# A decoder trunk on one core: Strassen's seven products for the merge of the three branches and for the down projection, and norms with one token per partition

## The chip, the cores and the metric

The kernel runs on one core of a Trainium2 chip. The metric is the device time of one execution in microseconds (us). All arithmetic is in f32.

## The reference, cut to what matters

Two layers of a decoder trunk for 512 prompt tokens and 8 sample tokens, D_MODEL 1024, D_FF 2816. What the change touches is the norm at the head of each layer and everything from the merge of the three branches (A, B, C) to the end of the layer:

```
h = rms_norm(x, norm_mix)
... the three token mixers make o_a, o_b, o_c from h @ w_in
m_a, m_b, m_c = split(sigmoid(h @ w_in[merge columns]), 3)
merged = m_a * (o_a @ w_rg_out) + m_b * (o_b @ w_gla_out) + m_c * (o_c @ w_nsa_out)
x = x + merged @ w_out
h = rms_norm(x, norm_ffn)
x = x + (silu(h @ w_ffn_gate) * (h @ w_ffn_up)) @ w_ffn_down
```

rms_norm divides each token by the root of the mean of its squares, plus 1e-6, and multiplies by a gain per channel.

## The kernel before, in words

Activations stand transposed: 1024 channels are 8 tiles of 128 partitions, and the free axis holds the 520 tokens (`xT`, `hT`, `oaT`, `obT`, `ocT`, each 128 x 8 x 520). PSUM holds 260 f32 tokens of a tile in a bank, so a tile is computed as two halves in a pair of banks. The two layers are one loop; a layer is a row of blocks, and between two blocks all engines meet. Weights come in slabs of 2 MB (1024 rows by 512 columns) into `ring`, which has three slots; SyncE's queue issues a slab's DMA (`load_slab`, L317) once TensorE has done with the slab three before it.

**Merge and output projection** (block from L2516). `proj_T` (L368) computes one tile of 128 channels by 520 tokens with 16 matmuls: 2 halves by 8 tiles of the inner dimension. There are 48 such tiles a layer: for each half of the columns, each branch and each of 4 tiles a gate tile from `hT` and an output tile from `oaT`, `obT` or `ocT`. ScalarE takes the sigmoid of the gate tile (L2549), VectorE multiplies the output tile by it (L2564) and adds it into `MG` (L2568). When all is merged, TensorE computes the 8 tiles of `w_out`; VectorE adds each into `xT` (L2571), ScalarE squares it (L569), and TensorE sums the squares over the channels with a matrix of ones, two matmuls a tile (`sum_tile`, L562), one tile behind.

**Norm.** The sums of squares stand in one pair of banks, the same on all 128 partitions. VectorE makes the means of them (L577), ScalarE the roots (L573), VectorE the reciprocals (L581) and the eight tiles of `hT` (L583), all as 128 x 520 operations. The norm at the head of a layer runs by the same lines in the first block of the layer, where squares and sums alternate.

**FFN** (block from L2580). Gate and up projection already go by Winograd's form of Strassen's algorithm. A step makes 2 tiles of channels by 520 tokens, with seven products P1 to P7 of 4 matmuls each (`product`, L457) instead of eight. VectorE makes four sums of weight blocks for each step, one step ahead (L467 to L472), and once four sums of blocks of `hT` (L477 to L482); ScalarE copies P1 from PSUM (L2615), and VectorE adds the products up (`add_products`, L489) as they end. Products go round the eight banks, so a product waits for the addition that read the bank eight products before. There are 22 steps a layer, then the down projection by plain matmuls (L2600), 352 program matmuls a layer, and VectorE adds each of 8 tiles into `xT` (L2652).

The order that sets how products and additions interleave is

```python
ORDER = ("P1", "P2", "P5", "P6", "P3", "P7", "P4")
```

The profile counts an f32 matmul of the program as two instructions of TensorE, with two weight loads.

## Time and profile before

| what | value |
|---|---|
| median of 3 runs | 3939.35 us (3935.71 to 3940.05) |
| the profiled execution's own time | 3938.83 us |
| its span, first to last instruction | 3937.2 us |
| TensorE busy | 3640.8 us, 92% of the span |
| VectorE busy | 1405.0 us, 36% |
| ScalarE busy | 761.7 us, 19% |
| mean granted TensorE clock | 0.945 |

The profile is of one execution. A row of the timeline gives the start in us from the first instruction, how long the merged instructions last together, engine, line, operation, output and inputs by the program's names, shapes, how many instructions (x), and in brackets how long the engine had been idle and what ended that. PEld is TensorE's weight load, DVE is VectorE, ACT is ScalarE. A line ending in "xN" with several instructions tells their common stretch, not one duration.

### The profile page before, as it was taken

The page shows a single profiled execution, that of the slowest core. Times are in us where ns is not written, and L with a number is a line of the kernel's source. Part 1 is how long each engine was busy: PE and PEld are TensorE (multiplying, and loading weights), DVE is VectorE, ACT ScalarE, POOL GpSimd, SP SyncE. Part 2 cuts the span into 40 slices and gives each one's busy share as a digit, 9 for nine tenths or more (in the row PEclk, how much of TensorE's full clock was granted, in tenths as well). Part 3 has the DMA queues.
Part 4 walks back from the last instruction along what each step waited for, and adds up shares of the span by engine and source line. Part 5 has one row for each costly group of instructions (what it writes and reads, how often), then busy time and mean ns, then how long its engine had stood idle before and what let it go on. Part 6 is the DMA issues. An engine that isn't in the chain of part 4 may idle for free. (4 is left out here: it accounts for less than half of the span.)

```text
span 3937.2 us, 47054 instructions
## 1 busy us (share of the span) xinstructions
PE 3640.8 (92%) x18570; PEld 2840.1 (72%) x18570; DVE 1405.0 (36%) x3043; ACT 761.7 (19%) x1564; POOL 285.9 (7%) x396
## 2 busy tenths in 40 slices
PE   6899898989789999999988988989887899999999
PEld 5777765755558887888877677556555688878888
DVE  4714514557300013442055164235662000144411
ACT  2312323146200001000032132221551000010000
POOL 0000011024200000000000000110342000000000
PEclk9999988989889999999999998889898999999999
DMA  4111353120542221222122104522206321212121
GB/s 141 46 65 44 101 153 118 59 114 1 169 136 71 86 83 46 86 75 91 38 100 67 64 27 131 161 75 75 97 16 192 113 77 65 86 65 86 65 102 38
DMA packets 222171, 336.97 MB, mean 86 GB/s; under 512 B 56614, under 2 KB 122386, under 8 KB 217210
## 3 DMA queue, kind: packets, MB, share of 16 engines
q1 hardware_dynamic: 204474, 281.91, 22.1%
q0 software_dynamic: 8064, 43.00, 3.1%
q10 hardware_dynamic: 9408, 8.98, 0.7%
q8 instruction: 151, 2.47, 0.3%
q14 instruction: 74, 0.61, 0.0%
HBM read 313.50 MB, written 37.10 MB: 89 GB/s over the span
## 5 line engine op out<-in xcount | busy, mean ns | idle before, releaser
L368 PE MATMUL pair<-hT,ring 128*128 128x260 f32 (+1 forms) x3648 | 835.2, 390 | 48.3 <-PEq L1419 25.2
L368 PEld LDWEIGHTS pair<-hT,ring 128*128 128x128 f32 (+1 forms) x3648 | 699.6, 192 | 171.6 <-issue 56.7
L383 PE MATMUL pair<-ring,hT 128*128 128x512 f32 (+2 forms) x800 | 311.8, 556 | 5.5 <-PEq L1262 5.5
L2600 PE MATMUL pair<-arena,ring 128*128 128x260 f32 x1408 | 309.1, 383 | 2.7 <-DVE arena L2648 2.7
L2600 PEld LDWEIGHTS pair<-arena,ring 128*128 128x128 f32 x1408 | 267.4, 190 | 44.4 <-DVE arena L2648 3.4
L383 PEld LDWEIGHTS pair<-ring,hT 128*128 128x128 f32 (+1 forms) x800 | 151.8, 212 | 153.4 <-issue 152.8
L2564 DVE TENSOR_TENSOR arena<-pair,arena 128x520 f32<-128x520 f32 x48 | 33.6, 700 | 626.4 <-PE pair L368 626.4
L457 PE MATMUL pair<-obT,oaT 128*128 128x260 f32 x1056 | 246.3, 383 | 0.0
L457 PEld LDWEIGHTS pair<-obT,oaT 128*128 128x128 f32 x1056 | 201.3, 191 | 31.2
L2118 POOL TENSOR_SCALAR arena<-arena 128x128 f32<-128x128 f32 (+3 forms) x256 | 152.4, 611 | 506.5 <-DVE arena L2077 506.5
L457 PE MATMUL pair<-hT,ring 128*128 128x260 f32 x704 | 169.4, 395 | 17.2 <-DVE hT L583 17.2
L457 PEld LDWEIGHTS pair<-hT,ring 128*128 128x128 f32 x704 | 137.8, 196 | 41.4 <-issue 16.4
L1529 PE MATMUL pair<-arena 128*128 128x512 f32 (+1 forms) x320 | 157.4, 578 | 6.6 <-DVE arena L1642 6.6
L489 DVE TENSOR_TENSOR ocT<-ocT,pair 128x260 f32<-128x260 f32 x220 | 91.2, 423 | 199.9 <-PE pair L457 194.5
L1983 ACT ACTIVATE arena<-arena 128x128 f32<-128x128 f32 (+3 forms) x256 | 141.4, 554 | 62.6 <-DVE arena L2037 60.6
L2549 ACT ACTIVATE arena<-pair 128x520 f32<-128x520 f32 x48 | 29.0, 604 | 621.2 <-PE pair L368 621.2
L1514 PEld LDWEIGHTS pair<-con,arena 128*128 128x128 f32 (+1 forms) x640 | 80.0, 153 | 76.4 <-issue 74.7
L880 POOL DMA_DIRECT2D out_p_gla_dram<-arena x8 | 4.6, 577 | 1728.2 <-DVE arena L1184 1728.2
L921 PE MATMUL pair<-hT,ring 128*128 128x260 f32 x512 | 125.6, 389 | 0.0
L2037 DVE CUSTOM_DVE_ANT_0 arena<-pair,con 128x128 f32<-128x128 f32 (+3 forms) x256 | 114.5, 484 | 28.8 <-PE pair L1912 28.6
L2652 DVE TENSOR_TENSOR xT<-pair,xT 128x520 f32<-128x520 f32 x16 | 11.2, 700 | 299.6 <-PE pair L2600 299.6
L368 PE MATMUL pair<-arena,ring 128*128 128x260 f32 x512 | 114.7, 383 | 3.0 <-DVE arena L2568 3.0
(372 smaller groups left out, 4922.5 us busy)
## 6 DMA issues: line engine op xcount, KB each, us to landing
ring<-in_w_in_dram SPq DMA_DIRECT2D x38, 2048.0 KB, 8.6
ring<-in_w_ffn_gate_dram SPq DMA_DIRECT2D x10, 2048.0 KB, 7.8
ring<-in_w_ffn_up_dram SPq DMA_DIRECT2D x10, 2048.0 KB, 7.8
ring<-in_w_ffn_down_dram SPq DMA_DIRECT2D x8, 2048.0 KB, 7.6
out_s_win_kv_dram<-in_cache_win_kv_dram SPq DMA_DIRECT2D x2, 8176.0 KB
...
```

What stands on the lines that cost most here:

```text
L368: last = pe.matmul(pair[o][0:m, half, 0:HA], lhs(k), rhs[:, k, half * HA:(half + 1) * HA], start=(k == 0), stop=(k == nk - 1))
L383: last = pe.matmul(big[0:rows, 0:w], hT[:, k, tt * P:tt * P + rows], slab[:, k, 0:w], start=(k == 0), stop=(k == KT - 1))
L457: last = pe.matmul(step_bank(q, prod), a[:, k, :], b[:, k, :], start=(k == 0), stop=(k == 3))
L489: dve.tensor_tensor(dst, a, step_bank(q, prod), op).then_inc(sem("st_sums"), 1)
L921: last = pe.matmul(pair[proj_pair(key)][:, half, 0:HA], gr[0][:, k, m % 4 * P:(m % 4 + 1) * P], hT[:, k, half * HA:(half + 1) * HA], start ...
L1514: last = pe.transpose(bank[4 + kv][:, g * P:g * P + n], R2[z // 2 % 3][0:n, kv * G + g, :], ident[0:n, 0:n])
L1529: pe.matmul(dst, PH[:, kv, 2 * qt + sp2_, :], src, start=(qt == 0 and sp2_ == 0), stop=(qt == 3 and sp2_ == 1)).then_inc(sem("ct_mm"), 1)
L1983: act.activation(s[:, u, 0:n], s[:, u, 0:n], ACT.Exp, bias=st[:, u:u + 1], scale=-1.0, accum_out=st[:, 4 + u:5 + u]).then_inc(sem("sa_e"), 1)
L2037: dve.tensor_tensor_reduce(out=SC[:, g % NSL, u, 0:n], in0=bank[S_BANK[u]][:, 0:n], in1=dist[:, 384 - i * P:384 - i * P + n], scale=SLOPE[ ...
L2118: pool.tensor_scalar(s, s, stat[:, g % NSL, 4 + u:5 + u], GATE[:, i, k:k + 1], ALU.mult, ALU.mult).then_inc(sem("sa_p"), 1)
L2564: dve.tensor_tensor(two(dst), both(proj_pair(key)), two(SG[i % 3]), ALU.mult).then_inc(sem("proj_read_dve"), 1)
L2600: last = pe.matmul(pair[m][:, half, 0:HA], w[:, k, m * P:(m + 1) * P], FA[:, r + k, half * HA:(half + 1) * HA], start=(r + k == 0), stop=( ...
```

## The change

- Merge and down projection become Strassen steps like those of the FFN: a layer has 24 merge steps (`MERGE_STEPS`), the 22 of gate and up as before, and 12 of the down projection (`DOWN_STEPS`), each the product of one slab of `w_ffn_down` (8, 8 or 6 tiles of rows) with a third of the activations, added straight into `xT`. Step, slab and input set follow from one list; the merge takes the branches one after the other.
- The sums stand in place: `T1` overwrites the block `B12` of its own input (so `input_sums` waits three times), and `stored_sums` builds U2, U5, U3 in the quarters of the destination. `added_sums`, for the down projection, has 11 additions a step, of them 4 of SBUF operands alone. Gates are taken by one 128 x 1040 operation behind the last sum, and the products with them too.
- Input sums are made once for each set: `hT` and `oaT` at the head of the merge, `obT` and `ocT` at steps 8 and 16, `hT` again behind the FFN norm, and three sets of the FFN's activations behind its steps of pairs 3, 7 and 10.
- Norms: VectorE adds up the eight squares (`add_square`), TensorE turns the sum with five matmuls of one column each, so that 128 tokens stand on the partitions; mean, root and reciprocal are 128 x 4 and 8 x 1; five matmuls with the identity spread the reciprocals over the partitions in PSUM (`spread_roots_pe`), from where VectorE reads them for `hT`.

```diff
+    MERGE_STEPS = [(n, hf, br, i) for br in range(3) for hf in range(2) for i in range(2) for n in ("mg", "mo")]
+    FFN_STEPS = [(n, i) for i in range(FT // 2) for n in ("fg", "fu")]
+    DOWN_STEPS = [("fd", hf, r, i) for hf in range(2) for r in range(0, FT, 8) for i in range(2)]
+    STEPS = MERGE_STEPS + FFN_STEPS + DOWN_STEPS
+    NTH = {key: q for q, key in enumerate(STEPS)}
+    SETS = ["hm", "oa", "ob", "oc", "hf", "f0", "f8", "f16"]
...
+    MADE_X = {"T3": 1, "T1": 2, "T2": 3, "T4": 4}
+    STORED = ("U2", "C11", "U5", "C12", "C22", "U3", "C21")
+    ADDED = ("X11", "U2", "C11", "U5", "C12", "X12", "C22", "U3", "X22", "X21", "C21")
...
+    def input_sums(dve, name, inputs):
+        x, xsum = inputs[name]
+        n, done = 4 * SETS.index(name), sem("st_inputs")
+        dve.tensor_tensor(xsum["T3"], input_block(x, "B22"), input_block(x, "B12"), ALU.subtract).then_inc(done, 1)
+        dve.wait_ge(done, n + MADE_X["T3"])
+        dve.tensor_tensor(xsum["T1"], input_block(x, "B12"), input_block(x, "B11"), ALU.subtract).then_inc(done, 1)
+        dve.wait_ge(done, n + MADE_X["T1"])
+        dve.tensor_tensor(xsum["T2"], input_block(x, "B22"), xsum["T1"], ALU.subtract).then_inc(done, 1)
+        dve.wait_ge(done, n + MADE_X["T2"])
+        dve.tensor_tensor(xsum["T4"], xsum["T2"], input_block(x, "B21"), ALU.subtract).then_inc(done, 1)
+    def input_tiles(x, space):
+        kh = x.shape[1] // 2
+        return x, {"T1": input_block(x, "B12"), **{t: space.take(kh, HA) for t in ("T3", "T2", "T4")}}
...
+    def stored_sums(dve, q, t):
+        c_ = quarters_of(t)
+        dve.wait_ge(sem("st_kept"), q + 1)
+        add_product(dve, q, "U2", c_["21"], c_["11"], "P6")
+        add_product(dve, q, "C11", c_["11"], c_["11"], "P2")
+        add_product(dve, q, "U5", c_["22"], c_["21"], "P5", made="U2")
+        add_product(dve, q, "C12", c_["12"], c_["22"], "P3", made="U5")
+        add_product(dve, q, "C22", c_["22"], c_["22"], "P7")
+        add_product(dve, q, "U3", c_["21"], c_["21"], "P7")
+        add_product(dve, q, "C21", c_["21"], c_["21"], "P4", ALU.subtract, made="U3")
+        dve.wait_ge(*sums_done(q, "C21"))
+    def added_sums(dve, q, t, u1, u2, u5):
+        c_, done = quarters_of(t), sem("st_sums")
+        dve.wait_ge(sem("st_kept"), q + 1)
+        dve.tensor_tensor(c_["11"], c_["11"], u1, ALU.add).then_inc(done, 1)
+        add_product(dve, q, "U2", u2, u1, "P6")
+        add_product(dve, q, "C11", c_["11"], c_["11"], "P2", made="X11")
+        add_product(dve, q, "U5", u5, u2, "P5", made="U2")
+        add_product(dve, q, "C12", c_["12"], c_["12"], "P3", made="U5")
+        dve.wait_ge(*sums_done(q, "C12"))
+        dve.tensor_tensor(c_["12"], c_["12"], u5, ALU.add).then_inc(done, 1)
+        add_product(dve, q, "C22", c_["22"], c_["22"], "P7")
+        add_product(dve, q, "U3", u2, u2, "P7")
+        dve.wait_ge(*sums_done(q, "C22"))
+        dve.tensor_tensor(c_["22"], c_["22"], u5, ALU.add).then_inc(done, 1)
+        dve.wait_ge(*sums_done(q, "U3"))
+        dve.tensor_tensor(c_["21"], c_["21"], u2, ALU.add).then_inc(done, 1)
+        add_product(dve, q, "C21", c_["21"], c_["21"], "P4", ALU.subtract, made="X21")
+    def keep_first(act, q, dst):
+        wait_product(act, q, "P1")
+        act.activation(dst, step_bank(q, "P1"), ACT.Copy).then_inc(sem("st_kept"), 1)
...
+    def norm_pe(pe, tag, ms):
+        pe.wait_ge(*normed(tag, "sum", KT - 1))
+        for tt, n in TOKENS:
+            last = pe.matmul(bank[6][0:n, tt:tt + 1], ms[:, tt * P:tt * P + n], ones[:, 0:1], start=True, stop=True)
+        last.then_inc(sem("norm_sum"), 1)
+    def spread_roots_pe(pe, tag):
+        pe.wait_ge(*normed(tag, "ms", 2))
+        for tt, n in TOKENS:
+            last = pe.matmul(bank[4 + tt // NT][:, tt % NT * P:tt % NT * P + n], rstd[0:n, 1, tt:tt + 1].to_broadcast([n, P]),
+                             ident[0:n, 0:n], start=True, stop=True)
...
+    def add_square(dve, tag, k, ms):
+        dve.wait_ge(*normed(tag, "sq", k + 1))
+        if k >= 2:
+            dve.wait_ge(*normed(tag, "sum", k - 1))
+        dve.tensor_tensor(ms, tag_sq[tag][0] if k == 1 else ms, tag_sq[tag][k % 2], ALU.add
+                          ).then_inc(sem("norm_sum"), 1)
...
+    def norm_mean(dve, own, tag):
         dve.wait_ge(*normed(tag, "sum", KT))
...
+        m, b = token_columns(rstd[:, 0, :]), token_columns(bank[6])
+        own.tick(dve.tensor_scalar(m[0], b[0], 1.0 / DM, EPS, ALU.mult, ALU.add))
+        own.wait()
+        dve.tensor_scalar(m[1], b[1], 1.0 / DM, EPS, ALU.mult, ALU.add).then_inc(sem("norm_ms"), 1)
+    def norm_dve(dve, own, tag, gain):
+        dve.wait_ge(*normed(tag, "rt", 2))
+        m, r = token_columns(rstd[:, 0, :]), token_columns(rstd[:, 1, :])
+        own(dve.reciprocal(r[0], m[0]))
+        dve.reciprocal(r[1], m[1]).then_inc(sem("norm_ms"), 1)
+        dve.wait_ge(*normed(tag, "sum", KT + 1))
+        both_banks = pair[2].rearrange("p a n -> p (a n)")[:, 0:TA]
         for k in range(KT):
-            dve.scalar_tensor_tensor(hT[:, k, :], xT[:, k, :], par[:, PR[gain] + k:PR[gain] + k + 1], ms,
+            dve.scalar_tensor_tensor(hT[:, k, :], xT[:, k, :], par[:, PR[gain] + k:PR[gain] + k + 1], both_banks,
...
+                for q in range(len(MERGE_STEPS)):
+                    open_slab(pe, step_slab(q))
+                    for prod in ORDER:
+                        product(pe, q, prod, wsum, inputs)
+                pe.wait_ge(sem("proj_read_dve"), dve_reads(MERGE_STEPS[-1]))
                 for hf in range(2):
                     w = open_slab(pe, f"wo{hf}")
                     for m in range(4):
                         j = 4 * hf + m
                         proj_T(pe, ("wo", j), lambda k: w[:, k, m * P:(m + 1) * P], MG)
...
+                norm_pe(pe, "ffn", ms8)
...
+                for q, (n, hf, br, i) in enumerate(MERGE_STEPS):
+                    if q >= 2 and (n == "mo" or br):
+                        act.wait_ge(sem("proj_read_dve"), dve_reads(MERGE_STEPS[q - 1 - (n == "mo")]))
+                    gate = MGATE if br else MG[:, 4 * hf + 2 * i:4 * hf + 2 * i + 2, :]
+                    keep_first(act, q, gate[:, 0, 0:HA] if n == "mg" else TMP[:, 0, 0:HA])
+                    if n == "mg":
+                        act.wait_ge(*sums_done(q, "C21"))
+                        act.activation(gate, gate, ACT.Sigmoid).then_inc(sem("proj_read_act"), 1)
...
+                weight_sums(dve, 0, wsum)
+                input_sums(dve, "hm", inputs)
+                weight_sums(dve, 1, wsum)
+                input_sums(dve, "oa", inputs)
+                for q, (n, hf, br, i) in enumerate(MERGE_STEPS):
+                    if 1 <= q < len(MERGE_STEPS) - 1:
+                        weight_sums(dve, q + 1, wsum)
+                    if q in (8, 16):
+                        wait_product(dve, q - 1, "P4")
+                        input_sums(dve, ("ob", "oc")[q // 8 - 1], inputs)
+                    merged = MG[:, 4 * hf + 2 * i:4 * hf + 2 * i + 2, :]
+                    gate = MGATE if br else merged
+                    stored_sums(dve, q, gate if n == "mg" else TMP)
+                    if n == "mo":
+                        dve.wait_ge(sem("proj_read_act"), act_reads(("mg", hf, br, i)))
+                        if br == 0:
+                            dve.tensor_tensor(merged, merged, TMP, ALU.mult).then_inc(sem("proj_read_dve"), 1)
+                        else:
+                            dve.tensor_tensor(TMP, TMP, MGATE, ALU.mult).then_inc(sem("merged"), 1)
+                            dve.wait_ge(sem("merged"), 4 * (br - 1) + 2 * hf + i + 1)
+                            dve.tensor_tensor(merged, merged, TMP, ALU.add).then_inc(sem("proj_read_dve"), 1)
                 for j in range(KT):
                     wait_proj(dve, ("wo", j))
                     dve.tensor_tensor(two(xT[:, j, :]), both(proj_pair(("wo", j))), two(xT[:, j, :]), ALU.add
                                       ).then_inc(sem("proj_read_dve"), 1)
+                    if j >= 2:
+                        add_square(dve, "ffn", j - 1, ms8)
+                add_square(dve, "ffn", KT - 1, ms8)
...
+                for q in range(len(MERGE_STEPS), len(STEPS)):
+                    n, *k = STEPS[q]
                     open_slab(pe, step_slab(q))
-                    product(pe, q, "P1", wsum, hT, xsum, made="ffn" if q == 0 else None)
-                    if q == 0:
+                    if q == len(MERGE_STEPS):
+                        product(pe, q, "P1", wsum, inputs, made="ffn")
                         pe.wait_ge(*normed("ffn", "h", KT))
+                    else:
+                        if n == "fd":
+                            pe.wait_ge(sem("proj_read_dve"), dve_reads(("fu", min(k[1] // 2 + 4, FT // 2) - 1)))
+                        product(pe, q, "P1", wsum, inputs)
                     for prod in ORDER[1:]:
...
+                        product(pe, q, prod, wsum, inputs)
...
+                norm_mean(dve, own, "ffn")
+                weight_sums(dve, len(MERGE_STEPS), wsum)
+                norm_dve(dve, own, "ffn", "ffn")
                 dve.wait_ge(*normed("ffn", "h", KT))
-                input_sums(dve, hT, xsum)
-                for q, (n, i) in enumerate(STEPS):
+                input_sums(dve, "hf", inputs)
+                for q in range(len(MERGE_STEPS), len(STEPS)):
+                    n, *k = STEPS[q]
                     if q + 1 < len(STEPS):
                         weight_sums(dve, q + 1, wsum)
...
+                    if n == "fg":
+                        stored_sums(dve, q, GATE)
+                    elif n == "fu":
+                        i, up = k[0], FA[:, 2 * k[0]:2 * k[0] + 2, :]
+                        stored_sums(dve, q, up)
                         dve.wait_ge(sem("proj_read_act"), act_reads(("fg", i)))
...
+                        dve.tensor_tensor(up, up, GATE, ALU.mult).then_inc(sem("proj_read_dve"), 1)
+                        if i in (3, 7, FT // 2 - 1):
+                            dve.wait_ge(sem("proj_read_dve"), dve_reads(("fu", i)))
+                            input_sums(dve, {3: "f0", 7: "f8"}.get(i, "f16"), inputs)
+                    else:
+                        j = 4 * k[0] + 2 * k[2]
+                        added_sums(dve, q, xT[:, j:j + 2, :], *KEPT)
```

TensorE at the end of a layer's merge and the start of the output projection before (`ocT` gives the output tiles of branch C, `arena` the merged `MG` and then the squares):

```order
L368 MATMUL pair<-hT,ring 128x260 x16
L368 MATMUL pair<-ocT,ring 128x260 x32
L368 MATMUL pair<-arena,ring 128x260 x32
L562 MATMUL pair<-arena,con 128x260 x2
L368 MATMUL pair<-arena,ring 128x260 x16
```

And now, from the last merge step on (`arena` in rows of L477 is sums of weights, `obT` sums of inputs, T1 stands in `ocT`):

```order
L477 MATMUL pair<-ocT,ring 128x260 x8
L477 MATMUL pair<-ocT,arena 128x260 x4
L477 MATMUL pair<-obT,arena 128x260 x4
L477 MATMUL pair<-ocT,arena 128x260 x4
L477 MATMUL pair<-obT,arena 128x260 x4
L477 MATMUL pair<-obT,ring 128x260 x4
L367 MATMUL pair<-arena,ring 128x260 x128
L624 MATMUL pair<-con,arena 128x1 x4
L624 MATMUL pair<-con,arena 8x1
```

A step of 28 matmuls has come for two tiles of 16, and the sums of squares have gone from between the tiles of the output projection to one short group behind them.

VectorE at the end of the merge and over the norm before the FFN, before:

```order
L2568 TENSOR_TENSOR arena<-arena 128x520
L2571 TENSOR_TENSOR xT<-pair,xT 128x520 x8
L2511 UNCONDITIONAL_BRANCH
L2622 UNCONDITIONAL_BRANCH
L577 TENSOR_SCALAR arena<-pair 128x520
L467 TENSOR_TENSOR oaT<-ring 128x512
L468 TENSOR_TENSOR oaT<-ring 128x512
L470 TENSOR_TENSOR oaT<-oaT,ring 128x512
L472 TENSOR_TENSOR oaT<-ring,oaT 128x512
L581 RECIPROCAL arena<-arena 128x520
L583 SCALAR_TENSOR_TENSOR hT<-xT,par,arena 128x520 x8
```

And now:

```order
L2672 TENSOR_TENSOR xT<-pair,xT 128x520
L645 TENSOR_TENSOR arena<-arena 128x520 x2
L2614 UNCONDITIONAL_BRANCH
L2718 UNCONDITIONAL_BRANCH
L664 TENSOR_SCALAR rstd<-pair 128x4
L666 TENSOR_SCALAR rstd<-pair 8x1
L487 TENSOR_TENSOR arena<-ring 128x512
L488 TENSOR_TENSOR arena<-ring 128x512
L490 TENSOR_TENSOR arena<-arena,ring 128x512
L492 TENSOR_TENSOR arena<-ring,arena 128x512
L671 RECIPROCAL rstd<-rstd 128x4
L672 RECIPROCAL rstd<-rstd 8x1
```

The four weight sums of the first FFN step still stand ahead of the reciprocals; one addition of squares has come behind the last tile.

## Rows read from the trace of the kernel before

**Rows 1.** The page: span, and busy time of each engine (share, instructions).

```profile
span 3937.2 us, 47054 instructions
PE 3640.8 (92%) x18570; PEld 2840.1 (72%) x18570; DVE 1405.0 (36%) x3043; ACT 761.7 (19%) x1564; POOL 285.9 (7%) x396
```

**Rows 2.** Windows: length, busy time by engine, granted clock, DMA share and GB/s.

```profile
1130.70:1136.00 5.30, 5.25 (x12) 4.21 (x13) 0.00 (x0) 1.15 (x1) 0.00 (x0) 0.50 0.77 259
1171.00:1470.00 299.00, 299.00 (x1366) 259.04 (x1364) 25.18 (x36) 12.69 (x21) 0.00 (x0) 1.00 0.25 78
1470.00:1480.00 10.00, 8.48 (x39) 7.20 (x39) 2.10 (x3) 0.22 (x1) 0.00 (x0) 1.00 0.59 210
1543.70:1552.00 8.30, 7.44 (x17) 5.38 (x17) 8.23 (x11) 1.67 (x2) 0.00 (x0) 0.50 0.00 0
1782.08:1794.35 12.27, 12.27 (x57) 10.64 (x56) 6.08 (x12) 1.02 (x2) 0.00 (x0) 1.00 0.27 85
1824.00:1974.70 150.70, 150.70 (x688) 130.34 (x686) 4.90 (x7) 0.00 (x0) 0.00 (x0) 1.00 0.12 41
```

**Rows 3.** Timeline, end of the first layer's merge and its output projection.

```profile
1470.24 0.70 DVE L2564 TENSOR_TENSOR arena<-pair,arena 128x520 f32<-128x520 f32 x1 [5.58 <-PE pair L368]
...
1470.97 0.70 DVE L2568 TENSOR_TENSOR arena<-arena 128x520 f32<-128x520 f32 x1
...
1471.73 14.29 PE L368 MATMUL pair<-arena,ring 128*128 128x260 f32 x64 [1.52 <-DVE arena L2568]
...
1486.06 0.70 DVE L2571 TENSOR_TENSOR xT<-pair,xT 128x520 f32<-128x520 f32 x1 [6.31 <-PE pair L368]
...
1493.95 0.70 DVE L2571 TENSOR_TENSOR xT<-pair,xT 128x520 f32<-128x520 f32 x1 [7.19 <-PE pair L368]
```

**Rows 4.** Timeline of VectorE in one Strassen step of the FFN.

```profile
1782.09 0.42 DVE L489 TENSOR_TENSOR ocT<-ocT,pair 128x260 f32<-128x260 f32 x1 [0.99 <-PE pair L457]
...
1784.35 0.69 DVE L472 TENSOR_TENSOR oaT<-ring,oaT 128x512 f32<-128x512 f32 x1
...
1794.36 0.42 DVE L489 TENSOR_TENSOR arena<-ocT,pair 128x260 f32<-128x260 f32 x1 [0.99 <-PE pair L457]
```

**Rows 5.** Timeline, norm before the FFN in the first layer.

```profile
1533.40 0.70 DVE L2571 TENSOR_TENSOR xT<-pair,xT 128x520 f32<-128x520 f32 x1 [7.19 <-PE pair L368]
...
1534.82 1.14 PE L562 MATMUL pair<-arena,con 128*128 128x260 f32 x4 [0.58 <-ACT arena L569]
...
1536.29 0.70 DVE L577 TENSOR_SCALAR arena<-pair 128x520 f32<-128x520 f32 x1 [2.19 <-PEq L2511]
...
1542.86 5.46 DVE L583 SCALAR_TENSOR_TENSOR hT<-xT,par,arena 128x520 f32<-128x520 f32 x8
...
1543.77 3.81 PE L457 MATMUL pair<-hT,ring 128*128 128x260 f32 x8 [7.81 <-DVE hT L583]
...
1549.51 1.23 DVE L478 TENSOR_TENSOR obT<-hT 128x1040 f32<-128x1040 f32 x1
```

**Rows 6.** Timeline, first layer's down projection, its start and its last addition.

```profile
1820.21 154.53 PE L2600 MATMUL pair<-arena,ring 128*128 128x260 f32 x704 [1.34 <-DVE arena L2648]
...
1974.78 0.70 DVE L2652 TENSOR_TENSOR xT<-pair,xT 128x520 f32<-128x520 f32 x1 [4.56 <-PE pair L2600]
```

**Rows 7.** Timeline, norm at the head of the second layer.

```profile
1984.88 1.16 ACT L569 ACTIVATE arena<-xT 128x520 f32<-128x520 f32 x2
...
1995.04 0.68 PE L666 MATMUL pair<-con,arena 32*128 32x32 f32 x8
...
1996.03 0.42 DVE L766 COPY arena<-pair 128x256 f32<-128x256 f32 x1
...
2000.89 5.54 PE L368 MATMUL pair<-hT,ring 128*128 128x260 f32 x12 [5.17 <-DVE hT L583]
...
2005.35 0.17 DVE L771 TENSOR_SCALAR arena<-arena 128x8 f32<-128x8 f32 x1
```

**Rows 8.** The page's DMA issues: KB each, median us to landing.

```profile
ring<-in_w_ffn_gate_dram SPq DMA_DIRECT2D x10, 2048.0 KB, 7.8
```

257 lines of the change are left out of this document (94 added, 163 removed).

## The prediction

> **What bounds the kernel now.** I read the page first: TensorE is busy 92% of the span, VectorE 36% [rows 1]. A share over stages proves nothing for the stages changed, so the windows come next: in the merge TensorE is busy all of 299 us, in the down projection all of 150.7 us, and in one Strassen step of the FFN all of 12.27 us, each at granted clock 1.00 [rows 2]. The reader is to see that TensorE waits for nobody inside these stages, so that there a matmul less is time less. Third, the timeline around their edges, where TensorE does wait: behind the merge, in the norms, ahead of the down projection. Those waits are what the change makes longer or shorter.
>
> **The price of a matmul.** A matmul of the program is two instructions in the profile. The merge's window has 1366 of them in 299.00 us [rows 2]: 438 ns for a matmul. The FFN's step has 28 matmuls in 12.27 us [rows 2, 4]: 438 ns as well. So a Strassen step runs at the full rate while VectorE is busy 6.08 us of its 12.27.
>
> **The sum**, against the profiled execution's own 3938.8 us (the median of the runs, 3939.35, is 0.5 us more, which I neglect). All for two layers.
>
> 1. Merge. 24 steps of 28 for 48 tiles of 16: 96 matmuls less a layer, 192 x 0.438 = -84.1.
> 2. Down projection. 7 x 4 x (4 + 4 + 3) = 308 matmuls for 352: 88 x 0.438 = -38.6. The 352 take 154.6 us now [rows 6], 439 ns each.
> 3. Sums of squares. Between two tiles of the output projection they take 7.89 instead of 7.01 us [rows 3] (16 matmuls at 438 ns), six times a layer: 12 x 0.88 = -10.6. The one-column matmuls that replace them are in the norm's chain (6).
> 4. Tail of the merge. Before, TensorE idles 1.52 us over two 0.70 us operations of VectorE [rows 3]. Now one quarter sum (0.42 [rows 4]) and a product and an addition of 128 x 1040 (1.23 each [rows 5], one waiting for the other) stand there, with some 0.25 of hand-overs: 3.15. Two times 1.6 = +3.2.
> 5. The clock behind that tail. Waits of 1.5 us [rows 3] and 1.3 us [rows 6] leave the next stretch at 1.00 (the window from 1470), but where the work ahead of a wait was thin the first 5.3 us of the merge ran at 0.50 [rows 2]. Nothing shows a wait of 3.15 us behind dense work. Bounds: nothing, or half of a stretch like the 8.3 us at 0.50 behind the FFN norm [rows 2], 4.2 us. I take a stretch of 3.4 at half, 1.7: twice = +3.4.
> 6. FFN norm, counted from the last tile's addition at 1533.40, from which the first product starts 10.4 us later now [rows 5]. In the change: addition and square 1.4 and the last sum of squares to 2.2; five one-column matmuls, ten instructions. For these bounds are 85 ns (eight small ones in 0.68 [rows 7]) and 0.28 us (four in 1.14 [rows 5]); at the nearer, weight-bound 0.16 it is 1.6, to 3.8; meeting of the engines 0.3; means 0.4 (0.17 each [rows 7] and a wait), to 4.5; then the four weight sums, which stay ahead, 2.5 (they end at 1785.04 behind an addition that ends at 1782.51 [rows 4]), to 7.1; two small reciprocals 0.4; spreading five times 128 columns, at half clock 2 x 438 x 128/260 = 0.43 each, 2.0, to 9.6; first tile of `hT` and start 0.9 [rows 5], to 10.6. So +0.2, twice = +0.4: the 3.4 us reciprocal goes, but the two passes through TensorE take its place, and VectorE's weight sums hide nothing of it. Between -1.5 and +1.5 each.
> 7. Start of the down projection. TensorE waits 1.34 us for VectorE now [rows 6]; the first down step needs only activations of pairs 0 to 3, long finished. Twice = -2.7. Its slab is issued when the pair 9 is done, a step ahead of the weight sums, and lands in 7.8 us [rows 8], under 12.27.
> 8. Last addition of a layer: 0.42 for 0.70 [rows 4, 6]: -0.6.
> 9. Norm at the head of a layer. From the first square to the first matmul it is 16.0 us [rows 7], in which TensorE sums at half speed beside ScalarE. Now: two squares 1.2, seven chained additions of 0.73 to 6.5, one-column matmuls 1.8, means 0.4; the parameters' turn and the copy of 0.42 that ends at 1996.45, 0.7 behind the start of the first [rows 7], to 10.1; reciprocals 0.4, spreading 2.1, first tile 0.9: 13.5. Twice -2.5 = -5.0. Between nothing, if the first slab of weights lands only then (it is requested among other loads), and -4 each.
>
> Sum: -84.1 - 38.6 - 10.6 + 3.2 + 3.4 + 0.4 - 2.7 - 0.6 - 5.0 = -134.6, so 3804.
>
> **What I cost at nothing.** VectorE's new work. A merge step has weight sums 2.5, seven additions 3.0 and, for an output, 2.5 of product and addition: 8 us of 12.27. A down step has 2.5 + 11 x 0.45 = 7.5 of 12.27, or 7 of 9.2 where it has 21 matmuls. The sets of input sums come on top, four of 1.23 to 1.27, 5.1 us: at merge steps 8 and 16 the order is 3.2 (tail of the step before) + 2.5 + 5.1 + 3.0 = 13.8, 1.5 us past the end of that step, but the first bank that waits for it is asked for two products into the next, 3.5 us in. At the head of the merge T1 is ready 2.5 + 2.5 = 5.0 us after the start, and P1 and P2 take 3.5 at full clock but 6 at the half clock that stands there [rows 2]; a wait of up to 1.6 is in the range. If this cover went, the price would be 5.1 at each set. The FFN's own steps stay as they are: additions in another order, a single 128 x 1040 operation (1.23) for two.
>
> A rule speaks against reading the reciprocals from PSUM. The rows have 0.70 for 520 columns both with a PSUM operand and for two SBUF ones (L2564 and L2568 [rows 3]), so I charge nothing. The Trainium skill (VectorE: DVE Perf Modes, the section on the TRN2 errata) gives a PSUM source 62 cycles of 0.96 GHz more than an SBUF source; by that, an estimate from this page, 4 norms x 8 tiles x 65 ns would add 2.1 us, for 3806.
>
> **Rivals.** (a) *Nothing is lost at the clock and the merge's head holds*: term 5 goes, 3801. For it: the two kept clocks behind dense work. (b) *The clock falls behind the merge's tail for as long as behind the FFN norm*: 4.2 for 1.7 us a layer, 3809. For it: a wait of 3.15 is twice any that left the clock whole; against: TensorE is dense on both sides of it. [...] (c) *VectorE is late where input sets change*: TensorE waits the whole 5.1 us at each of five sets a layer (steps 8 and 16, pairs 3, 7 and 10), 51 us, 3855. Against it: the reckoning above has 2 us to spare at the worst. (d) *Slower: VectorE becomes the bound.* Additions now write the quarters that the next addition reads, so each waits for the last, and a bank is free only when its addition is done. The 72 changed steps (48 and 24) win 123 us on TensorE, 1.7 a step; so VectorE decides from 12.27 + 1.7 = 14 us a step, 5 more than its 8 to 9, which is 0.4 more for each of 13 instructions. At twice its length, 17 us, it would be 72 x 3 = 216 us over the kernel before, 4155. Against it: the FFN's chain, whose additions wait for each other too, keeps 0.42 [rows 4] at 6.08 us of 12.27. That the change does not do what it says is out: the order on TensorE has 28 matmuls a step.
>
> **Chances.** The forecast, within 3 us, 0.55; (a) 0.17; (b) and other waits of a few us 0.18; (c), whole or in part, 0.06; (d) 0.03; a gain beyond (a) 0.01. The range: from below, (a) with the norms at their lower bounds, 3801 - 8 = 3793; from above, (b) with the head's wait of 1.6 and the FFN norm's upper bound, twice, 3809 + 6 = 3815. That leaves out (c), (d) and little else. Faster by over 0.2% (some 8 us, which is about what a measurement of this kernel can tell from no change): 0.96; within it 0.01; slower 0.03.
>
> **What would show it.** TensorE's matmul instructions fall by 2 x (192 + 88) = 560 and by 128 for the squares, with 40 small ones added; the last additions of successive merge steps 12.27 us apart; a wait of 3.1 us at the output projection and then its granted clock, 1.00 or 0.50; 10.6 us from the last tile to the FFN's first product; no wait ahead of the down projection; 13.5 us in the other norm. The prediction is wrong if in steps 8, 16 or behind pairs 3, 7 and 10 TensorE is idle, or if a step takes more than 12.27 us.

## The result, and the profile after

The changed kernel takes 3802.09 us (median of 4 runs, 3800.29 to 3806.30), the kernel before, beside it, 3938.40: ratio 0.9656, 95% interval 0.9639 to 0.9673. The forecast was 3804 (3793 to 3815). The profiled execution's own time is 3803.26, 135.6 us below the 3938.8 of before. From here on, brackets behind a measured time hold its ratio to the kernel before, run beside it, and the 95% interval of that ratio. The page of the changed kernel:

```profile
span 3801.6 us, 47446 instructions
PE 3500.4 (92%) x17962; PEld 2719.8 (72%) x17962; DVE 1856.3 (49%) x3945; ACT 780.3 (21%) x1594; POOL 285.5 (8%) x396
```

TensorE is 140 us less busy [rows 1], and VectorE 451 us more: half the span now, and still not the bound. The 608 instructions less are the 560 and 128 of the forecast less 80 small ones (I wrote 40: each small matmul, too, is two). Windows of the changed kernel, columns as in [rows 2]: the head of the merge, one merge step, the output projection's start, the end of the FFN norm with the first products behind it, the down projection, and the head norm of layer 2.

```profile
1131.28:1134.69 3.41, 3.41 (x10) 2.64 (x9) 3.34 (x6) 0.63 (x2) 0.00 (x0) 0.50 0.82 212
...
1203.00:1215.27 12.27, 12.27 (x58) 10.64 (x57) 6.44 (x13) 0.39 (x1) 0.00 (x0) 1.00 0.00 0
1431.65:1435.07 3.42, 3.42 (x9) 2.69 (x9) 0.00 (x0) 0.00 (x0) 0.00 (x0) 0.50 0.88 329
1493.09:1503.33 10.24, 6.40 (x18) 4.79 (x18) 7.48 (x13) 1.16 (x5) 0.00 (x0) 0.50 0.26 96
...
1772.77:1908.04 135.27, 135.00 (x616) 116.70 (x615) 80.19 (x181) 4.65 (x12) 0.00 (x0) 1.00 0.16 55
...
1912.93:1936.83 23.90, 10.63 (x40) 9.04 (x41) 11.80 (x23) 10.94 (x17) 0.00 (x0) 0.50 0.77 256
```

A merge step keeps TensorE busy for all of its 12.27 us, beside 6.44 us of VectorE; the down projection has 616 instructions, two for each of its 308 matmuls, in 135.27 us. The other four rows are stretches at clock 0.50, to which I come back. The timeline at the merge's tail and in the FFN norm answers to [rows 3, 5]:

```profile
1427.25 0.42 DVE L519 TENSOR_TENSOR arena<-arena,pair 128x260 f32<-128x260 f32 x1 [0.99 <-PE pair L477]
1427.71 1.24 DVE L2667 TENSOR_TENSOR arena<-arena 128x1040 f32<-128x1040 f32 x1
1428.98 1.24 DVE L2669 TENSOR_TENSOR arena<-arena 128x1040 f32<-128x1040 f32 x1
...
1430.28 10.06 PE L367 MATMUL pair<-arena,ring 128*128 128x260 f32 x37 [3.07 <-DVE arena L2669]
...
1488.38 0.70 DVE L2672 TENSOR_TENSOR xT<-pair,xT 128x520 f32<-128x520 f32 x1 [5.71 <-PE pair L367]
...
1490.54 1.18 PE L624 MATMUL pair<-con,arena 128*128 128x1 f32 x10 [2.20 <-DVE arena L645]
1492.01 1.28 ACT L656 ACT_TABLE_LOAD   x1 [2.26 <-PEq L2614]
1492.05 0.16 DVE L664 TENSOR_SCALAR rstd<-pair 128x4 f32<-128x4 f32 x1 [1.56 <-PEq L2614]
...
1494.86 0.17 DVE L671 RECIPROCAL rstd<-rstd 128x4 f32<-128x4 f32 x1
...
1495.27 2.60 PE L631 MATMUL pair<-con,rstd 128*128 128x128 f32 x10 [3.55 <-DVE rstd L672]
...
1498.81 1.21 PE L477 MATMUL pair<-hT,ring 128*128 128x260 f32 x2 [0.94 <-DVE hT L676]
```

TensorE waits 3.07 us at the tail; from the last tile to the first FFN product it is 10.43 us. Ahead of the down projection the 1.34 us of [rows 6] are gone. At the other norm, the head of layer 2, which answers to [rows 7]:

```profile
1916.67 1.16 ACT L638 ACTIVATE arena<-xT 128x520 f32<-128x520 f32 x2
...
1917.87 0.70 DVE L645 TENSOR_TENSOR arena<-arena 128x520 f32<-128x520 f32 x1 [9.40 <-ACT arena L638]
...
1918.61 1.16 ACT L638 ACTIVATE arena<-xT 128x520 f32<-128x520 f32 x2 [0.77 <-DVE arena L645]
...
1919.28 4.73 DVE L645 TENSOR_TENSOR arena<-arena 128x520 f32<-128x520 f32 x6 [0.70 <-ACT arena L638]
...
1924.06 1.99 PE L624 MATMUL pair<-con,arena 128*128 128x1 f32 x10 [16.28 <-DVE arena L645]
...
1926.32 1.06 PE L759 MATMUL pair<-con,arena 32*128 32x32 f32 x8
...
1927.70 0.43 DVE L862 COPY arena<-pair 128x256 f32<-128x256 f32 x1
...
1928.58 2.60 PE L631 MATMUL pair<-con,rstd 128*128 128x128 f32 x10 [1.20 <-DVE rstd L672]
...
1932.12 0.77 PE L367 MATMUL pair<-hT,ring 128*128 128x260 f32 x1 [0.94 <-DVE hT L676]
```

First square to first matmul: 15.45 us, of which 13.5 were forecast. Both traces, cut at the same events (us, layer 1 / layer 2):

| segment | before | after | change, two layers | forecast |
|---|---|---|---|---|
| head norm, first square to first matmul | 15.87 / 16.00 | 15.45 / 15.44 | -1.0 | -5.0 (term 9) |
| to the merge's first matmul (untouched) | 1078.71 / 1078.42 | 1078.79 / 1079.49 | +1.2 | 0 |
| merge to the first addition of the output projection | 348.29 / 348.52 | 308.56 / 308.56 | -79.7 | -77.5 (terms 1, 4, 5) |
| output projection, first to last addition | 54.35 / 54.35 | 49.09 / 49.09 | -10.5 | -10.6 (term 3) |
| FFN norm, last addition to first product | 10.37 / 10.37 | 10.43 / 10.43 | +0.1 | +0.4 (term 6) |
| first product to the last addition of the layer | 431.71 / 431.83 | 409.66 / 409.66 | -44.2 | -41.9 (terms 2, 7, 8) |
| to the first square of layer 2 | 9.41 | 8.21 | -1.2 | 0 |

The sum is -135.3, for the 135.6 measured. The untouched stage before the merge differs by up to 9.6 us between layers and kernels below; medians of 3 to 5 runs move with it, so effects of a few us are read from these segments.

### The profile page after: what moved, and what is told of

Its sections match the earlier page's. It is cut to its first block and busy times, and to the rows that moved or that the text cites. A ratio compares the mean times of both kernels' runs of the same rounds, so it can differ in the third digit from the quotient of the medians.

```text
span 3801.6 us, 47446 instructions
## 1 busy us (share of the span) xinstructions
PE 3500.4 (92%) x17962; PEld 2719.8 (72%) x17962; DVE 1856.3 (49%) x3945; ACT 780.3 (21%) x1594; POOL 285.5 (8%) x396
## 3 DMA queue, kind: packets, MB, share of 16 engines
q10 hardware_dynamic: 9408, 8.98, 0.7%
## 5 line engine op out<-in xcount | busy, mean ns | idle before, releaser
L367 PE MATMUL pair<-hT,ring 128*128 128x260 f32 (+1 forms) x2112 | 484.1, 391 | 36.7 <-PEq L1515 25.1
L367 PEld LDWEIGHTS pair<-hT,ring 128*128 128x128 f32 (+1 forms) x2112 | 402.5, 191 | 113.5 <-issue 46.4
L519 DVE TENSOR_TENSOR arena<-arena,pair 128x260 f32<-128x260 f32 x490 | 188.8, 421 | 406.9 <-PE pair L477 405.8
L477 PE MATMUL pair<-hT,ring 128*128 128x260 f32 x1088 | 257.4, 391 | 6.3 <-DVE hT L676 3.4
L477 PE MATMUL pair<-hT,arena 128*128 128x260 f32 x1088 | 260.8, 383 | 1.2 <-DVE hT L500 1.2
L477 PE MATMUL pair<-oaT,arena 128*128 128x260 f32 x1056 | 253.6, 382 | 0.0
L477 PEld LDWEIGHTS pair<-hT,ring 128*128 128x128 f32 x1088 | 210.7, 194 | 41.5 <-issue 5.2
L477 PEld LDWEIGHTS pair<-hT,arena 128*128 128x128 f32 x1088 | 206.4, 190 | 33.8 <-issue 2.0
L477 PEld LDWEIGHTS pair<-oaT,arena 128*128 128x128 f32 x1056 | 200.7, 190 | 30.8
L477 PE MATMUL pair<-arena 128*128 128x260 f32 x864 | 207.6, 382 | 0.0
L477 PEld LDWEIGHTS pair<-arena 128*128 128x128 f32 x864 | 164.2, 190 | 25.2
L477 PE MATMUL pair<-arena,ring 128*128 128x260 f32 x608 | 142.4, 382 | 0.0
L477 PE MATMUL pair<-oaT,ring 128*128 128x260 f32 x592 | 140.8, 382 | 0.0
L477 PEld LDWEIGHTS pair<-arena,ring 128*128 128x128 f32 x608 | 115.5, 190 | 17.7
```

What stands on the lines that cost most here:

```text
L367: last = pe.matmul(pair[o][0:m, half, 0:HA], lhs(k), rhs[:, k, half * HA:(half + 1) * HA], start=(k == 0), stop=(k == nk - 1))
L477: last = pe.matmul(step_bank(q, prod), a[:, k, :], b[:, k, :], start=(k == 0), stop=(k == kh - 1))
L519: dve.tensor_tensor(dst, a, step_bank(q, prod), op).then_inc(sem("st_sums"), 1)
```

## The experiments

**Down projection as before** (16 plain matmuls per tile and slab, one addition per tile):

```
-    STEPS = MERGE_STEPS + FFN_STEPS + DOWN_STEPS
+    STEPS = MERGE_STEPS + FFN_STEPS
...
+                pe.wait_ge(sem("proj_read_dve"), dve_reads(STEPS[-1]))
+                for hf in range(2):
+                    for r in range(0, FT, 8):
+                        w = open_slab(pe, f"fd{hf}{r}")
```

> The changed kernel (3802.1) with the down projection by plain matmuls again. My theory, that TensorE bounds every step, gives back 88 matmuls at 0.438 (38.6), the wait ahead of the down projection (2 x 1.3) and 2 x 0.3 of the last addition: 3844, between 3840 and 3848. The rival, that VectorE's 7.5 us a down step already costs TensorE part of the gain, gives less than 38 back, so under 3838.

Measured: 3847.93 us (ratio 0.9786, 0.9768 to 0.9805), 46 above the change; the FFN and the down projection take 431.12 and 432.80 us, as before the change. TensorE waits again ahead of the down projection, 1.88 us in layer 1 and 1.89 in layer 2. The two timelines, and a window behind each:

```profile
1768.85 1.33 PE L2711 MATMUL pair<-arena,ring 128*128 128x260 f32 x5 [1.88 <-DVE arena L2751]
...
3675.95 1.51 PE L2711 MATMUL pair<-arena,ring 128*128 128x260 f32 x5 [1.89 <-DVE arena L2751]
```
```profile
1767.00:1772.00 5.00, 3.15 (x15) 2.78 (x16) 1.67 (x2) 0.00 (x0) 0.00 (x0) 1.00 0.68 231
...
3676.98:3680.39 3.41, 3.41 (x10) 2.65 (x9) 0.00 (x0) 0.00 (x0) 0.00 (x0) 0.50 0.92 354
```

The same wait left the clock at 1.00 in one layer and lowered it for 3.4 us in the other.

So terms 2, 7 and 8 belong to this part, with 44.6 us by the segments and 46 by the medians; the time is at the upper edge of what I gave, and far from the rival's 3838. No run puts the merge's plain tiles back: what its steps win is read from the segment of the table alone.

**Norms as before** (ones-matrix matmuls over each square, a 128 x 520 reciprocal):

```
+                        if j:
+                            sum_tile(pe, "ffn", j - 1)
...
+    def norm_dve(dve, own, tag, ms, gain):
+        dve.wait_ge(*normed(tag, "rt", 1))
+        own(dve.reciprocal(ms, ms))
```

> The changed kernel with the old norms (sums of squares on TensorE over 520 columns). By my terms the norm part wins 10.6 by the sums of squares between the output projection's tiles, and by the trace of the changed kernel 0.5 for each norm at the head of a layer and nothing before the FFN: 3802 + 11.5 = 3814, between 3810 and 3817. If the one-token-per-partition norms themselves won the 2.5 each that I forecast at the heads, it would be 3818.

Measured: 3809.81 (0.9688, 0.9671 to 0.9706), 7.7 above the change. By segments: output projection 54.35 (+5.26 a layer), FFN norm 10.37, head norm 17.00 and 16.73 (+1.55 and +1.29). The sum of these is 13 us; in the profiled execution the untouched stage was 10.9 us shorter, and the median stands just under the range that I gave. What the new norms win lies nearly all in the output projection, where TensorE no longer sums; the norms' own chains are no shorter than before in the FFN and little shorter at the head. The old head norm also varies, 15.87 to 17.00 us in the two kernels that have it, while the new one is 15.43 to 15.45 in each layer of the kernels that leave it as it is.

**The tail's wait removed.** The first tile of the output projection sums its first six products of each half before it waits for the merge's last output:

```
+                        for ks in (range(6), range(6, KT)):
+                            if ks[0]:
+                                pe.wait_ge(sem("proj_read_dve"), dve_reads(MERGE_STEPS[-1]))
+                            for half in range(2):
+                                for k in ks:
```

> The first tile of the output projection multiplies the six merged tiles that are long finished, and only then waits for the last two. The wait of 3.07 us shrinks to some 0.5 (the 12 matmuls before it take 5.3 us at 438 ns, so it may go altogether). Theory that the wait itself lowers the granted clock for 3.4 us behind it: the stretch stays at 1.00, and each layer wins 3.07 + 1.7 = 4.8, so 3792.6. Rival, the clock falls for another reason (the merge's load or its length): 3.1 each, 3796, with a stretch at 0.50 still there.

Measured: 3796.98 (0.9649, 0.9634 to 0.9664).

```profile
1431.74 4.55 PE L2641 MATMUL pair<-arena,ring 128*128 128x260 f32 x20
1431.94 0.43 DVE L519 TENSOR_TENSOR arena<-arena,pair 128x260 f32<-128x260 f32 x1 [0.99 <-PE pair L477]
```

TensorE goes from the last product straight into the projection, at clock 1.00 in both layers. Merge to first addition falls by 3.95 us in layer 1 and 5.02 in layer 2: the wait of 3.07, and some 1.7 that the clock had cost, less 1.1 in layer 1, where the clock at the merge's head was low for 5.6 us behind the first product. The median is nearer to the rival's 3796 than to 3792.6, and its interval overlaps that of the change; what decides between them is the clock, which the rival had at 0.50. The medians cannot, for a part of the gain went again behind the FFN norm: in layer 2 that norm took 10.73 us for 10.43 and the stage behind it 411.01 for 409.66, 1.65 more.

**The tail's wait filled** with six matmuls whose results nobody reads:

```
+                pe.wait_ge(*sums_done(len(MERGE_STEPS) - 2, "C21"))
+                for _ in range(6):
+                    pe.matmul(bank[0][:, 0:HA], ident, xT[:, 0, 0:HA], start=True, stop=True)
```

> The wait stays, but TensorE does six matmuls of 260 columns in it whose results nobody reads (2.6 us of the 3.07). If idleness lowers the clock, the stretch at 0.50 behind the tail goes and nothing else changes: 1.7 each, 3798.7, wait still ending at the same addition. If the clock has another reason, 3802 and the stretch stays.

Measured: 3800.03 (0.9667, 0.9649 to 0.9685).

```profile
1428.53 2.79 PE L2627 MATMUL pair<-xT,con 128*128 128x260 f32 x12
1431.76 2.46 PE L367 MATMUL pair<-arena,ring 128*128 128x260 f32 x10 [0.44 <-DVE arena L2672]
```

The projection starts when it did, the clock stays at 1.00 in both layers, and merge to first addition is 306.87 in both, 1.69 less than with an idle TensorE. That is the 1.7 of term 5. In layer 1 the clock at the merge's head was 1.00 as well, P1 and P2 were done sooner, and TensorE waited 1.45 us for T1. This is the wait of up to 1.6 us that I had allowed for, and the prediction's numbers have it where it came, at the full clock: 3.5 us of products against 5.0 for T1, but 6 at the half clock.

In layer 2 this run lost 1.65 us behind the tail as well, in the FFN norm (11.01) and the stage behind it (410.73), where the clock was low for 17.06 us; in the change it was low for 10.24 there.

```profile
3366.00:3383.06 17.06, 11.81 (x36) 9.32 (x36) 12.34 (x20) 3.25 (x5) 0.00 (x0) 0.50 0.29 111
```

Two of the four layers of these two runs lost that much; of the four kernels that keep both the wait and this FFN norm, with their eight layers, one layer lost 0.8 and the others nothing. Whether the one comes of the other is not shown by so few; what a filled tail wins in its segment is not yet won in the whole.

**Reciprocals ahead of the weight sums** in the FFN norm:

```
-                weight_sums(dve, len(MERGE_STEPS), wsum)
-                norm_dve(dve, own, "ffn", "ffn")
+                norm_dve(dve, own, "ffn", "ffn", lambda: weight_sums(dve, len(MERGE_STEPS), wsum))
```

> In the FFN norm VectorE takes its two reciprocals ahead of the four weight sums, so that ScalarE's roots and TensorE's spreading start as soon as the means are there, and the weight sums (2.6 us in the changed kernel's trace) run while TensorE spreads (2.6 us). In the changed kernel the spreading waits for reciprocals that stand behind the weight sums: TensorE starts it 3.2 us behind the means. Theory 1 (the sum's term 6: the weight sums stand in the norm's chain and hide nothing): last output-projection addition to first FFN product falls from 10.43 to about 8.9 to 9.2 us in both layers, -1.2 to -1.5 each, so 3799.5 us against 3802.1 of the change. Theory 2 (the weight sums merely fill a wait for something else, TensorE's half clock or ScalarE's roots): the segment stays within 0.3 us of 10.43 and the time at 3802.

Measured: 3805.27 (0.9674, 0.9655 to 0.9693), no difference in the whole that can be told from the change, and above the 3799.5 expected; the segment is 9.21 in both layers for 10.43.

```profile
1489.69 1.28 ACT L656 ACT_TABLE_LOAD   x1 [2.25 <-PEq L2616]
1489.73 0.16 DVE L664 TENSOR_SCALAR rstd<-pair 128x4 f32<-128x4 f32 x1 [1.56 <-PEq L2616]
...
1490.99 0.30 ACT L656 ACTIVATE rstd<-rstd 128x4 f32<-128x4 f32 x2
1491.32 0.18 DVE L671 RECIPROCAL rstd<-rstd 128x4 f32<-128x4 f32 x1 [1.24 <-ACT rstd L656]
```

Theory 1 holds, with less to win than the sums' own 2.6 us: behind them hid ScalarE's load of a table, 1.28 us, which is next in the chain. In this execution some 0.8 of the 1.22 went again: the clock was low until 8.0 us (layer 1) and 8.2 us behind the first product, 4.5 in the change, and the stage behind the norm took 410.46 and 410.56 us for 409.66. A layer with the norm as in the change shows the same 0.8 (layer 1 of the run with late copies below), so it is not shown to belong to the edit.

**Parameters in the head norm, twice.** First, the transposes ahead of the one-column matmuls and the copies behind the reciprocals:

```
-                norm_pe(pe, "mix", ms0)
                 pe.wait_ge(sem("par_in"), PAR_IN)
...
                 last.then_inc(sem("par_turned"), 1)
+                norm_pe(pe, "mix", ms0)
...
-                norm_dve(dve, own, "mix", "mix")
+                norm_dve(dve, own, "mix", "mix", parameters)
```

`parameters` holds VectorE's two copies, and `norm_dve` calls it behind its reciprocals.

> In the norm at the head of a layer the parameters' transposes stand ahead of the one-column matmuls on TensorE, where it idles 16 us for the chained sums anyway, and VectorE's two copies of them stand behind its reciprocals. Theory 1 (what missed the forecast of 13.5 us there is the chain of small operations behind the eight summed squares: one-column matmuls, parameters, reciprocals, spreading, each in turn): first square to first matmul falls from 15.45 to between 13.8 and 14.5 us, 3799 to 3800.5 us. Theory 2 (the first slab of weights lands only then, and bounds the norm from below): it stays at 15.4, whatever is taken from the chain, and the time at 3802.

Measured: 3801.32 (0.966, 0.9643 to 0.9677), head norm 16.46 and 16.86: longer, a miss of both theories.

```profile
1928.83 0.41 PE L758 MATMUL pair<-con,arena 88*128 88x88 f32 x1 [17.65 <-DMA kgain<-in_nsa_k_norm_g_dram]
```

The last parameter lands 8.8 us behind the first square (at 1920.06 there), and now everything waits for it. Then the copies alone (the last pair of lines above):

> As the changed kernel, but in the norm at the head of a layer the two copies of the parameters stand behind VectorE's reciprocals, while the transposes of the parameters stay where they were, behind the one-column matmuls (put ahead of them they waited for the last parameter, which landed 8.8 us after the first square, and the norm grew from 15.45 to 16.5 and 16.9 us). Theory 1 (the chain behind the eight summed squares sets the end): reciprocals at once behind ScalarE's roots, spreading behind the parameters' transposes: first square to first matmul 14.2 to 14.4 us for 15.45 in both layers, -2.3 us in all. Theory 2 (the landing of something, the weights or the parameters, sets it): it stays at 15.4.

Measured: 3803.52 (0.967, 0.9656 to 0.9684), head norm 14.25 and 14.24.

```profile
1924.35 0.18 DVE L671 RECIPROCAL rstd<-rstd 128x4 f32<-128x4 f32 x1 [0.36 <-ACT rstd L656]
...
1924.86 2.60 PE L631 MATMUL pair<-con,rstd 128*128 128x128 f32 x10
```

-1.2 in each layer: the chain of small operations set the end there, as theory 1 had it. The first slab of weights landed before it, 13.3 and 11.9 us behind the first square.

**How far VectorE's cover goes.** The four weight sums once more in every step; or three times more in the merge's 24 steps alone:

```
+        for _ in range(3 if q < len(MERGE_STEPS) else 0):
+            for x in ("S1", "S2", "S3", "S4"):
+                dve.tensor_tensor(wsum(q, x), weight_block(q, "A21"), weight_block(q, "A22"), ALU.add
+                                  ).then_inc(sem("more_sums"), 1)
...
+            dve.wait_ge(sem("more_sums"), more[0])
```

> VectorE forms the four sums of weights a second time in every one of the steps of merge, FFN and down projection (same sources, same targets, so the result stands): 2.5 us more of a step's 12.27, in all some 58 x 2 x 2.5 = 290 us more work of VectorE, which then is busy some 9 us of 12.27. Theory 1 (TensorE bounds every step and VectorE's cover is wide, as the sum took it): the time moves by at most 3 us a layer, at the FFN norm and at the start of the stages, where the sums stand in the chain: 3802 to 3812. Theory 2 (the cover is thin, and the change was near rival (d)): TensorE waits in the steps, 1 us or more in each, so 3900 or more.

> In the 24 merge steps alone VectorE forms the four sums of weights three times more, 7.5 us more a step. VectorE is busy 6.6 us of 12.27 in a merge step of the changed kernel, and with its starts and hand-overs about 7, so 14.4 to 14.6 are asked of it in 12.27. Theory 1 (rival (d)'s rule: from the point where VectorE's work of a step passes 12.27, each step takes what VectorE takes): 2.1 to 2.4 us x 24 x 2 = +100 to +115, so 3900 to 3920, the steps 14.4 us apart. Theory 2 (an addition that waits for the last one costs more than its own length once VectorE has no slack): the steps are 16 us apart or more, 3980 and up. Theory 3 (banks and slabs give slack that hides it): under 3850.

Measured: once more, 3814.0 (0.9698, 0.9678 to 0.9717); three times more in the merge, 3927.39 (0.9984, 0.9974 to 0.9994). Ten merge steps of the first, then of the second the whole merge, one pair of steps (gate and output) of branch A and one of branch B:

```profile
1200.00:1322.70 122.70, 122.70 (x561) 106.39 (x560) 91.70 (x162) 9.11 (x15) 0.00 (x0) 1.00 0.24 77
```
```profile
1127.75:1485.43 357.68, 313.66 (x1344) 263.48 (x1344) 343.02 (x585) 22.07 (x37) 0.00 (x0) 0.95 0.23 71
...
1213.48:1240.60 27.12, 25.08 (x113) 21.12 (x113) 26.36 (x48) 1.73 (x3) 0.00 (x0) 1.00 0.14 47
...
1301.08:1329.47 28.39, 25.08 (x112) 21.12 (x112) 27.59 (x49) 1.73 (x3) 0.00 (x0) 0.99 0.31 110
```

At 9.2 us of VectorE in a step TensorE waits in none of the ten; what it costs lies where the sums stand in a chain: +2.5 in each FFN norm, +3.6 and +4.8 at the merge (its head waits for T1), +1.1 and +1.2 behind the norm. These are 15.7 us; the medians show 12, and 3814 is 2 us more than I allowed. With three more sets VectorE is busy 343 of 357.7 us, TensorE 313.7, and merge to first addition grows by 61.2 and 62.9 us. The pairs show how: 27.12 us a pair in branch A and 28.39 in B and C, 13.6 and 14.2 a step, of which VectorE is busy 13.2 and 13.8. Over 12.27 that is 41 us in 24 steps; a pair in which an input set is made takes 5.0 more, twice, as no slack hides it any longer; and some 10 stand at the head, where two sets and the added sums delay the first products. So theory 1 is right in its rule, though 3927 lies above its 3900 to 3920: I had the steps at 14.4 to 14.6, which is too long, and had left out the sets and the head. At 9.2 us of VectorE a step costs what TensorE takes, at 13.2 and more what VectorE takes and 0.4 on top, with no penalty of 16 us a step; between the two no run stands.

**Together**, the split first tile, the early reciprocals and the late copies:

> Three edits together: the first tile of the output projection sums its first six products of each half before it waits for the merge's last output; the FFN norm's reciprocals ahead of the weight sums; the head norm's copies behind the reciprocals. By the segments of the runs that had one each: -4 to -5 us a layer at the merge's tail, -1.22 in the FFN norm, -1.1 in the head norm, so -13 to -15 against the changed kernel's 3802.1: 3788 (3785 to 3792). If the parts are not independent (the clock falls somewhere else for a wait that is shorter), less: 3793 or more.

Measured: 3791.07 (0.9637, 0.9624 to 0.9651). Segments: head 14.26 and 14.24, merge 303.54 twice, FFN norm 10.02 and 9.32. This beats both kernels, the changed one by 11 us in the medians (the intervals still overlap a little) and by 14 in these segments, less 1.35 in the stage behind the FFN norm of layer 1. The FFN norm got less of its 1.22: in layer 1 the clock fell right behind the last tile, at 1483.07, for 17.1 us, and the one-column matmuls ran at 0.50.

**The norms with idle matmuls** on top of that, 20 or 9 of them at the start of the head norm:

```
+                idle_work(pe, 20, 0)
+                for n in range(2, KT - 1):
+                    pe.wait_ge(*normed("mix", "sum", n))
+                    idle_work(pe, 1, 0)
                 norm_pe(pe, "mix", ms0)
```

> As the run with three edits together, and in the norms TensorE does matmuls whose results nobody reads: 4 ahead of the one-column matmuls, 4 ahead of the spreading, 1 behind it in the FFN norm; 20 behind the down projection (or the start), one at each of the sums of squares 2 to 6, one behind the spreading in the head norm. Theory 1 (the small matmuls of a norm are dear because the granted clock there is 0.50): with the clock kept at 1.00 spreading takes 1.3 us for 2.6, the one-column matmuls of the head 1.2 for 2.0, and the first products after a norm run at full speed: -1.3 and what the first 4 us behind a norm gain in the FFN norm, -2.5 and as much in the head norm of layer 2; in all -8 to -14 us, 3774 to 3780. Theory 2 (small matmuls cost what they cost at any clock, and added work delays the chain as much as it warms): within 3 us of the run without them, 3788.

> As the run with three edits and idle matmuls, but with 9 instead of 20 of them at the start of the head norm, where 25 in a row held up the one-column matmuls (50 instructions in 13.51 us, the first 4.65 us of them at granted clock 0.50) so that the norm took 15.9 and 16.1 us. Theory 1 (the granted clock sets what the small matmuls of a norm cost): one-column matmuls 1.1 us for 2.0, spreading 1.5 for 2.6, the parameters' transposes 1.0 for 1.5: first square to first matmul falls from 14.25 to 12.0 to 12.8 us in layer 2, and as much or less in layer 1, where the clock has to rise first; 3784 to 3787 us for 3788 with 20 and 3791 with none. Theory 2 (what the idle matmuls win they cost again in the chain): the norm stays at 14 us or more.

Measured: 3788.23 (0.9625, 0.9611 to 0.9639) with 20, 3791.35 (0.9625, 0.9612 to 0.9639) with 9. With 20, in layer 2:

```profile
1911.71 13.51 PE L683 MATMUL pair<-con 128*128 128x260 f32 x50 [6.83 <-issue]
1925.06 1.07 PE L624 MATMUL pair<-con,arena 128*128 128x1 f32 x10
...
1927.29 1.47 PE L631 MATMUL pair<-con,rstd 128*128 128x128 f32 x10 [0.32 <-DVE rstd L672]
```

At clock 1.00 spreading takes 1.47 for 2.60 us and the one-column matmuls 1.07 for 1.99: theory 1 is right about the price. But the time did not go to its 3774 to 3780; it is within 3 us of the run without idle work, as theory 2 had it, and the intervals overlap. The idle work itself began at 0.50 and held the norm up (15.85 and 16.13). With 9 that delay is gone, and the norm still takes 14.30 and 15.45. What TensorE's weight loads wait for there, in layer 2:

```profile
PEld pair L367 <- DMA ring<-in_w_in_dram: 2.5, 1, 2.5
```

The first slab of weights, issued at 1916.67 behind the parameters, lands 9.6 us later, at 1926.3, and the first matmul starts at 1926.35. In layer 1 it lands 14.26 us behind the first square, 0.04 ahead of the first matmul. So theory 2's number came (14 us or more), but not by its cause: what the clock wins, the slab takes. Nor did the clock win all there was: in layer 2 it was low again from 1920.22, and spreading took 2.60 us. In the FFN norm idle work gives 8.98 for 9.21.

## Why the prediction was right, point by point

- **The total**: right within 1 us, and that is in part luck, as misses cancel. Term 9 won 4.0 less than forecast and the untouched stage cost 1.2; against these stand 2.2 more in the merge, 2.3 more in the FFN's stage and 1.2 ahead of the next layer's first square, none of which I had a term for.
- **What bounds the kernel**: right. In steps of full rate a matmul less was 0.438 us less. The merge steps are 12.27 us long, and term 3 came within 0.1; the merge segment won 2.2 more than forecast, of which some 1.9 is its head: the clock was low there for 3.41 us, not 5.3 [rows 2], which terms 1 to 9 had taken as it was. That is luck too: in the kernels above the clock was low there for 0 to 6.0 us behind the first product.
- **Terms 2, 7, 8**: 44.2 for 41.9. The wait of 1.34 went, the last addition is a quarter sum of 0.43 us, and the down projection takes 135.27 for 154.6. The 2.3 more lie in the FFN's own steps, 273.96 for 275.10 a layer: the low clock reaches less far into the products behind the norm (to 1503.33 from a first product at 1498.81, 4.5 us, against at least 8.2 before [rows 2, 5]), half of which difference is 1.9 a layer, less 0.6 of a wait for T1 that appeared in its place, for 1.15 a layer measured. I had no term for it.
- **Term 4**: 3.07 for 3.15. **Term 5**: this execution had exactly the stretch that I chose, 3.4 us at 0.50 in both layers; that was luck in part. Over the eight kernels that kept the wait of 3.07 us, the clock fell behind it in 11 of 16 layers, and stayed at 1.00 in 5. Filling the wait gave 1.69 back, which is the price that I had set at 1.7. Rival (a) is right in the 5 cases, rival (b)'s 4.2 in none; the longest stretch was one of 6.8 us, which costs 3.4. The Trainium skill (TensorE: Matmul & The Clock Gate, the section on oscillation) describes a kernel whose waits of some 3 to 5 us between groups of matmuls send the clock back each time. At 3.07 us the rows agree with it in 11 of 16. Shorter waits inside dense work (of [rows 3, 6], of the merge steps with VectorE overloaded, and ahead of the plain down projection) show it less: of seven between 2.80 and 2.87 us four lowered the clock, of five between 1.88 and 2.11 us two, of eleven between 1.04 and 1.75 us none. All seven of 3.8 to 7.9 us in the merge with VectorE overloaded came with a low clock.
- **Term 6**: 10.43 for 10.6, though two of its parts were off and cancelled: one-column matmuls 1.18 for 1.6, spreading 2.60 for 2.0. That the weight sums stand in the chain was right, as the run without them there showed (9.21); that nothing else would be late behind them was not said, and was the table load.
- **Term 9** is the one that failed: -1.0 for -5.0. Behind the first square I had 13.5 and it was 15.45. The chained additions end at 7.3, not 6.5 (1.2 and seven times 0.73 are 6.3, so my sum had already 0.2 too much). The squares have two buffers, so the third waits for the first addition, and the second addition for the third square: VectorE is idle 0.70 us ahead of it. The later ones follow each other at 0.80, not 0.73. One-column matmuls at the low clock take 2.0 (+0.2), the parameters' turn and copies 0.25 more, spreading 2.6 (+0.5). Nor would 13.5 have paid in full in layer 2: the first slab landed at 1930.96 (issued at 1922.16, 8.8 us), 14.3 us behind the first square; in layer 1 it was 13.1. The prediction had named this as its bound, and then took its value without asking when the slab is issued.
- **Cost at nothing**: right but for the first FFN step, where TensorE waits 0.77 us for `hT`, as it did before (0.80), and 0.62 for T1. No other step of merge, FFN or down projection has TensorE waiting, at the input sets neither; rival (c) is out. Rival (d)'s rule was shown by loading VectorE until it came true; the change stands at 6.4 to 6.9 us of 12.27 and is far from it.
- **PSUM source**: the eight tiles that read their factor from PSUM take 5.42 us (L676, both norms), those that read it from SBUF 5.46 [rows 5]. The 2.1 us of the rule (the Trainium skill, VectorE: DVE Perf Modes, the section on the TRN2 errata) did not appear; the measurement decides.
